# Attention branch product of a hybrid decoder layer: three products of 264 columns a tile become products of 400, 264 and 128 columns

## The reference

```
z = h @ w_in            # q, k, v, u, gate_a, gate_s
att = dilated attention of three head groups, merged      # 512 wide
merged = (jax.nn.sigmoid(gate_a) * (att @ p['w_attn_branch'])
          + jax.nn.sigmoid(gate_s) * (s_out @ p['w_ssm_branch']))
x = x + merged @ p['w_out']
```

## Time and profile before

| | |
|---|---|
| median of 3 executions | 2341.26 us (2337.91 to 2343.0) |
| profiled execution, first to last instruction | 2338.9 us |
| TensorE busy in it | 2285.7 us (98%) |
| `attn_branch`, from A0's first product to its last | about 1384.9 to 1410.0 us |

### The profile page before, as it was taken

One profiled execution on the slowest core, in us unless ns is written; L12 is line 12 of the kernel. 1 busy time (PEld: TensorE's weight loads), 2 busy tenths in 40 slices (PEclk: granted clock), 3 DMA queues, 4 the chain that ended last, 5 costly groups with the idle time before them and its releaser, 6 DMA issues.

```text
span 2338.9 us, 47519 instructions
## 1 busy us (share of the span) xinstructions
PE 2285.7 (98%) x18583; PEld 2264.1 (97%) x18583; DVE 1402.5 (60%) x1416; ACT 982.2 (42%) x1213; POOL 539.1 (23%) x571
## 2 busy tenths in 40 slices
PE   8999999999999999899999999999999999999999
PEld 7899999999999998898999999999999999999999
DVE  5575457775455656776655777665555455544555
ACT  5434334333334543333445556444343344433432
POOL 4793026660000204654403650010000000000000
PEclk9999999999999999999999999999999999999999
DMA  8779777777787677647948767567887787757764
GB/s 238 238 224 308 226 239 247 259 262 238 233 250 215 207 241 236 199 147 231 307 153 282 274 187 227 180 193 246 251 248 226 237 249 241 228 180 232 243 197 138
DMA packets 434774, 535.55 MB, mean 229 GB/s; under 512 B 27832, under 2 KB 415920, under 8 KB 430824
## 3 DMA queue, kind: packets, MB, share of 16 engines
q1 hardware_dynamic: 419600, 511.55, 69.7%
q0 software_dynamic: 3408, 11.75, 1.5%
q10 hardware_dynamic: 11664, 10.84, 1.4%
HBM read 510.85 MB, written 109.00 MB: 265 GB/s over the span
## 4 chain that ended last, share of the span: by engine, by line
PE 81%; POOL 8%; DMA 5%; DVE 3%; issue 2%; ACT 1%; SPq 0%; DVEq 0%; ACTq 0%; POOLq 0%
PE pa L1231 26%; PE pa L1232 25%; PE pa L1233 25%; DMA qb<-q_dram 3%; POOL silu_v L1733 2%; POOL c_exp L1678 1%; POOL pre L1674 1%; POOL qk L1735 1%; POOL qk L1737 1%; DVE w_lo L862 1%; ACT w_hi L562 1%; DVE head_sd L998 1%; DMA raw<-in_ffn_w_gate 1%; DMA raw<-in_ffn_w_up 1%; PE pb L1317 1%
## 5 line engine op out<-in xcount | busy, mean ns | idle before, releaser
L862 DVE TENSOR_TENSOR w_lo<-raw,w_hi 128x1024 fp32r<-128x1024 f32 x736 | 933.8, 1281 | 678.3 <-ACT w_hi L562 673.4
L1231 PE MATMUL pa<-xg_hi,w_hi 128*128 128x264 f32 x3968 | 1138.4, 287 | 10.6 <-DVE w_lo L862 10.5
L1232 PE MATMUL pa<-xg_lo,w_hi 128*128 128x264 f32 x3968 | 1131.7, 285 | 0.0
L1233 PE MATMUL pa<-xg_hi,w_lo 128*128 128x264 f32 x3968 | 1129.9, 285 | 0.0
L562 ACT ACTIVATE w_hi<-raw 128x1024 fp32r<-128x1024 f32 x736 | 766.4, 1054 | 757.1 <-PE pa L1233 711.6
L1231 PEld LDWEIGHTS pa<-xg_hi,w_hi 128*128 128x128 f32 x3968 | 751.5, 189 | 15.7 <-issue 9.8
L1232 PEld LDWEIGHTS pa<-xg_lo,w_hi 128*128 128x128 f32 x3968 | 749.9, 189 | 0.2
L1233 PEld LDWEIGHTS pa<-xg_hi,w_lo 128*128 128x128 f32 x3968 | 750.1, 189 | 0.0
L1232 PE MATMUL pa<-act_lo,w_hi 128*128 128x264 f32 x1632 | 463.8, 284 | 0.0
L1231 PE MATMUL pa<-act_hi,w_hi 128*128 128x264 f32 x1632 | 463.5, 284 | 0.0
L1233 PE MATMUL pa<-act_hi,w_lo 128*128 128x264 f32 x1632 | 463.1, 284 | 0.0
(11 more groups left out here) (304 smaller groups left out, 1661.2 us busy)
## 6 DMA issues: line engine op xcount, KB each, us to landing
raw<-in_ffn_w_gate SPq DMA_DIRECT2D x172, 512.0 KB, 4.8
raw<-in_ffn_w_up SPq DMA_DIRECT2D x172, 512.0 KB, 5.4
out_kv_s<-in_cache_kv_w SPq DMA_DIRECT2D x165, 512.0 KB
raw<-in_ffn_w_down SPq DMA_DIRECT2D x160, 512.0 KB, 4.4
raw<-in_w_in SPq DMA_DIRECT2D x152, 512.0 KB, 4.9
raw<-in_w_out SPq DMA_DIRECT2D x32, 512.0 KB, 4.5
tab<-ssm_tab SPq DMA_DIRECT2D x8, 1664.0 KB, 9.3
raw<-in_w_ssm_branch SPq DMA_DIRECT2D x16, 512.0 KB, 4.4
```

Source lines behind the costliest of these rows:

```text
L862: dve.tensor_tensor(w_lo[:, slot], raw[:, slot], w_hi[:, slot].bitcast(f32), ALU.subtract).then_inc(lo_ready, 1)
L1231: pe.matmul(out, wh, hi, start=first, stop=False)
L1232: pe.matmul(out, wh, lo, start=False, stop=False)
L1233: return pe.matmul(out, wl, hi, start=False, stop=last)
```

## The change

The high and the low half of the attention output stand side by side in one buffer `att_x` (columns 0 to 263 high, 264 to 527 low). A tile is now: `w_hi` times columns 0 to 399, written to 400 columns of the bank; `w_lo` times the high half, 264 columns; `w_hi` times columns 400 to 527, added into columns 136 to 263 of the bank. So the low half's first 136 columns end up apart from the rest, in columns 264 to 399 of the bank. VectorE puts them together: it copies them to `gate_v`, adds columns 0 to 135 of the bank, and multiplies by the gate in two pieces.

```diff
+WIDE = 400
-    att_hi, att_lo = tiles(RT + 8 * T, 32 * T, ("att_hi", [P, NSLOT, T], f32r), ("att_lo", [P, NSLOT, T], f32r))
+    att_x = tile("att_x", [P, NSLOT, 2 * T], f32r, RT + 8 * T)
...
-                        act.activation(att_hi[:], att_v[:], ACT.Copy).then_inc(att_hi_ready, 1)
+                        act.activation(att_x[:, :, 0:T], att_v[:], ACT.Copy).then_inc(att_hi_ready, 1)
...
-                        dve.tensor_tensor(att_lo[:], att_v[:], att_hi[:].bitcast(f32), ALU.subtract).then_inc(att_lo_ready, 1)
+                        dve.tensor_tensor(att_x[:, :, T:2 * T], att_v[:], att_x[:, :, 0:T].bitcast(f32), ALU.subtract).then_inc(att_lo_ready, 1)
...
                     dve.wait_ge(slab_used, ph.slab(i, g)[2] + 1)
                     dve.wait_ge(sig_ready, c + 1)
-                    dve.tensor_tensor(gates[:, 2 * c:2 * c + 2, :], pa[:, b:b + 2, 0:T], gates[:, 2 * c:2 * c + 2, :],
+                    dve.wait_ge(evacuated, ph.group(i, g))
+                    dve.tensor_copy(gate_v[:, :, 0:WIDE - T], pa[:, b:b + 2, T:WIDE]).then_inc(att_low, 1)
+                    dve.wait_ge(att_low, 2 * c + 1)
+                    dve.tensor_tensor(gate_v[:, :, 0:WIDE - T], pa[:, b:b + 2, 0:WIDE - T], gate_v[:, :, 0:WIDE - T], ALU.add).then_inc(att_low, 1)
+                    dve.tensor_tensor(gates[:, 2 * c:2 * c + 2, WIDE - T:T], pa[:, b:b + 2, WIDE - T:T], gates[:, 2 * c:2 * c + 2, WIDE - T:T], ALU.mult)
+                    dve.wait_ge(att_low, 2 * c + 2)
+                    dve.tensor_tensor(gates[:, 2 * c:2 * c + 2, 0:WIDE - T], gate_v[:, :, 0:WIDE - T], gates[:, 2 * c:2 * c + 2, 0:WIDE - T],
                                       ALU.mult).then_inc(evacuated, 1)
...
-                    slab_products(ph, i, g, g, att_hi, att_lo, 0, KS, True, True)
+                    slot, turn, n = ph.slab(i, g)
+                    pe.wait_ge(lo_ready, n + 1)
+                    b = 2 * ph.banks(i, g)
+                    for c in range(2):
+                        for kk in range(KS):
+                            wh, wl = w_hi[:, slot, kk, P * c:P * c + P], w_lo[:, slot, kk, P * c:P * c + P]
+                            pe.matmul(pa[:, b + c, 0:WIDE], wh, att_x[:, kk, 0:WIDE], start=kk == 0, stop=False)
+                            pe.matmul(pa[:, b + c, 0:T], wl, att_x[:, kk, 0:T], start=False, stop=False)
+                            ins = pe.matmul(pa[:, b + c, WIDE - T:T], wh, att_x[:, kk, WIDE:2 * T], start=False, stop=kk == KS - 1)
+                    ins.then_inc(slab_used, 1)
```

More of the change, by code:

```diff
@@ L339, in build_layer @@
     xnew_step, st_t, st_rows_ready = sems("xnew_step st_t st_rows_ready")
-    att_hi_ready, att_lo_ready, sig_ready, prod_s, m_ready, x_back = sems("att_hi_ready att_lo_ready sig_ready prod_s m_ready x_back")
+    att_hi_ready, att_lo_ready, att_low, sig_ready, prod_s, m_ready, x_back = sems("att_hi_ready att_lo_ready att_low sig_ready prod_s m_ready x_back")
     yt_ready, yrow_ready, stored = sems("yt_ready yrow_ready stored")
```

## The result

The changed kernel takes 2344.21 us as the median of 18 executions, against 2339.8 us for 18 of the kernel before beside them. The ratio is 1.0018, with a 95% interval of 1.001 to 1.0025: slower by about 4.2 us (2.3 to 5.9). The forecast was +3.3 us and 2344.6 us. That 2344.6 is so near to 2344.21 is in part luck: it was added to a median of three, 2341.26, which is 1.5 us above the median of 18.

What follows compares the result with a forecast made beforehand. TensorE's rows of products bound attn_branch, with VectorE deciding its end. TensorE's part of 3.3 us and longer evictions, walked through the end, gave +3.3 us, 2344.6 us; 8 in 10 range 2340.8 to 2348.5.

Steps and rivals of the forecast that it cites:

- The likeliest case: Whole kernel: the forecast itself, +3.3 us, spanning 2.4 to 3.9 us, chance 0.65.
- A tile: Three products at the high clock: 0.178 + 0.121 + 0.112 = 0.411 us (0.390 to 0.425), against 0.363 before.
- The floor of a load under the short product: 128-column product: the weight load and not the columns sets its price, 0.112 us, between 0.109 and 0.121.
- TensorE's part: Products of attn_branch: 59 x 0.048 + 0.5 = 3.3 us added (2.1 to 4.2).
- The term for the low clock: Start of attn_branch: the short product costs about 0.22 us there, 0.11 more a tile over 5 tiles, some 0.5 us.
- The evictions: VectorE: four instructions replace one of 0.71 us, about 1.65 us in all, +0.94 for each eviction.
- In A0 to A5 it is hidden: First six slabs of attn_branch: longer evictions cost nothing, as VectorE needs 2.88 us a slab and a slab lasts 3.29.
- the reopening of banks is hidden: PSUM banks in attn_branch: later reopening costs nothing, since a group is reopened a whole slab later.
- The end of the phase: Handover behind attn_branch: G0 starts without its old 0.9 us wait, G1 waits for zs_lo until about 1417.05, +3.3 us.
- the rate of plain float32: Rival on the short product: it costs 0.22 us, a tile 0.519, +9.4 us, 2350.7 us; chance 0.14.
- Loads don't get hidden behind the long product: Denies a rival: long product hides the short one's load, tile 0.363 us or less, +1.8 us, 2343.1 us; chance 0.12.
- VectorE does not bound the changed kernel: Denies a rival: evictions take 2.4 us, VectorE's slab 3.65 against TensorE's 3.29, +4.8 us, 2346.1 us; chance 0.07.

Runs made afterwards that it cites:

- e1: The changed kernel with the wide product cut from 400 to 272 columns, so a tile has 272, 264 and 256; 2340.55 us, ratio 1.0001 to the kernel before.
- e2: The changed kernel with the wide product widened from 400 to 512 columns, so a tile has 512, 264 and 16; 2346.59 us, ratio 1.0037 to the kernel before.
- e4: The changed kernel with its products of 400, 264 and 128 columns, but the old one-instruction eviction; 2344.01 us, ratio 1.0021 to the kernel before.
- e5: The changed kernel with the one-instruction eviction and the wide product cut to 264 columns, the short one still 128; 2341.03 us in one execution.
- e6: The changed kernel with the short product second, so a tile runs 400, 128, 264 columns; 2345.86 us in one execution.
- e3: The kernel before with only the four-instruction evictions of the change, TensorE's products as before; 2341.32 us, ratio 1.0007.

## Why the prediction was right

**The size.** Forecast +3.3 us; by the timed runs +4.2 (2.3 to 5.9), by the trace +2.9. The trace's figure lies within the forecast's own 2.4 to 3.9, and the interval of the timed one holds 3.3, though 4.2 itself lies above 3.9. The likeliest case came true, and none of the rivals. The mechanism was right, and e1, e2, e4 and e5 show it; the nearness of the absolute time is in part luck, as said.

**A tile.** Forecast 0.411 us (0.390 to 0.425), measured 0.415. The floor of a load under the short product was right: 0.112 forecast, 0.115 in e5. It also grows as it should with the width (e1, e2). The long product is nearer to its upper end: with 0.121 for the 264-column product and 0.112 for the short one, 0.415 leaves 0.182, against 0.178 taken. What was wrong is the picture of the starts that I said would prove it, "0.17 to 0.18, 0.12 and 0.11 apart": they were 0.24, 0.12 and 0.06. The sum holds, but by that sign alone one could have thought the short product cheap and the long one dear. e5 and e6 exclude that, and the forecast distances stand in the starts of the loads. The rule that the next load starts with the product ahead of it holds only where that product isn't itself waiting for its load: in e2 the load at 1402.58 comes 0.11 behind the one before it, at 1402.47, and 0.09 behind the product's recorded start, 1402.49.

**TensorE's part.** Forecast 3.3 us. From A0's first product to the place where G0 can start it was 24.95 us before (1409.81 - 1384.86) and 28.19 after: +3.2. The term for the low clock was near: +0.11 a tile (0.77 against 0.66), over 4 tiles rather than 5.

**The evictions.** Forecast 1.65 us each, measured 1.59. The forecast's own terms add up to less than it wrote: 1.73 + 0.04 - 2 x 0.08 = 1.61. Its 2.88 us for VectorE's slab also leaves out the overlaps of `w_lo` with its neighbours; e3 has 2.65. "In A0 to A5 it is hidden" was right for this kernel, because its slabs are 3.32 us long. e3 shows that the cover is thin: with slabs of 2.91 us, `w_lo` at up to 1.98 us beside it and evictions of 1.6 or more, TensorE waited for its banks twice. I had said that the reopening of banks is hidden without pricing that case.

**The end of the phase.** The forecast had G0 at 1413.1 without a wait and G1 at 1417.05 after one of about 1 us. It was G0 at 1413.73 and G1 at 1417.35 in an execution that began the phase 0.68 later; less that, 1413.05 and 1416.67. The wait ahead of G1 was 0.7 us by the starts, since VectorE's last six steps, from `w_lo` of G1 to the second half of `zs_lo`, took 7.71 us (1409.59 to 1417.30) and not 8.1: the evictions were 0.06 shorter each, and the walk added up whole durations where neighbours overlap by some 0.08.

**The rivals.** The short product does not fall back to the rate of plain float32: e5 gives 0.115, not 0.22. The evidence for that was weaker than the prediction says: its 16 "short products" at L1483 are 8 products in the kernel (4 x 2), with plain float32 operands and two records each, so 0.112 was the price of a record with its load. It carried over because the reduced type has one record a product (192 records for the phase's 192 products). Loads don't get hidden behind the long product: slabs are 3.32 us and not 2.91. What the page TensorE: Matmul & The Clock Gate of the Trainium skill says in its section on LDWEIGHTS, from which 107 ns follow for 128 columns, agrees with 0.11 between two loads here. Its formula for the back-to-back issue gap, taken alone for the short product, does not. The prediction left out what that section says beside the formula: that it is for a single product and counts too little for few columns, as it holds no load. The section gives about 81 ns for 128 columns in a stream of loads and products; here it is 0.11 us. VectorE does not bound the changed kernel, but it holds TensorE up at two slabs once TensorE is as fast as before (e3).

## What to carry to other kernels

In a row of products like these, each with a load of its own, a product costs at least that load, here 0.11 us. A piece of 256 columns was still free of it (e1), one of 128 was not: cutting a moving operand into unequal pieces with the same number of products gained nothing at any of the widths tried, and lost as soon as a piece was that short. Count the products, not only the columns. Where a neighbouring engine hands over at the end of a phase, walk its queue in order before pricing a longer step: a wait of 0.9 us took up part of the loss, and the longer evictions made a new one behind it.

## What the runs showed of the hardware that was not expected

- The distance from one product's recorded start to the next can hold the rest of a load: 0.24 us for 400 columns behind a short product, 0.18 behind a 264-column one (e6). The distance between load starts did not have this: 0.18 for 400 columns in both orders.
- The low clock at the start of the phase differs between executions of nearly the same instructions: the first slab took 1.65 us more than one in the middle of the phase in the kernel before, 2.5 in e1, 3.0 in e6 and 0.1 in e3, where the granted clock stayed at 1.00. That is some 3 us of scatter, as much as the change costs. TensorE waited 2.2 us ahead of A0 each time.
- `w_lo` took up to 1.98 us in the first slabs of the phase and 1.22 later. In the same stretch GpSimd works, and its own instructions are uneven too. In e3:

```profile
1391.50 1.61 POOL L1825 TENSOR_TENSOR xtmp<-a_t,x_t 128x256 f32<-128x256 f32 x1
1393.18 0.74 POOL L1826 TENSOR_TENSOR xtmp<-a_t,x_t 128x256 f32<-128x256 f32 x1
```

  The first overlaps `w_lo` (1390.53 to 1392.51), the second mostly an eviction. GPSIMD Engine Reference of the Trainium skill states in its section on specifications that the two engines share their way to SBUF, and get in each other's way when VectorE's instruction has two SBUF inputs, as `w_lo` has. These rows fit that, but not every row does: in e1 a `w_lo` beside a GpSimd instruction of 1.69 us took 1.21. No run here took GpSimd's work away, so the cause is argued only.
